# Second half's front in four slots a step of one tile each, with numbered beats and a third weight buffer

## The chip, the cores and the metric

The kernel runs on one core of a Trainium2 chip. Its time is that of one launch, in microseconds of the device. The core has TensorE (PE, matrix products into PSUM), VectorE (DVE), ScalarE (ACT), GpSimd (POOL) and SyncE (SP, here only a queue that issues DMAs), which run on their own and wait for each other by semaphores. All DMAs share 16 DMA engines.

## What is computed

One layer of a hybrid model over a prompt of 512 tokens and 8 single-token samples, D = 1024, float32.

```
h = modulate(rmsnorm(x), sh1, sc1);  proj = h @ w_in        -> u, z, xbc, dt, gates
ya = s5_branch(u);  ya = ya * sigmoid(ya @ w_glu + b_glu)   # "glu"
xs, B, C = silu(causal_conv(xbc))                           # "x": 2048 columns, 4 taps
yb = ssd(xs, dt, B, C, state)                               # chunks of 128 tokens; samples: one step each
yb = group_rmsnorm(yb * silu(z))
x  = x + gt1 * ((sigmoid(gA) * (ya @ w_branch_a) + sigmoid(gB) * (yb @ w_branch_b)) @ w_out)
h2 = modulate(rmsnorm(x), sh2, sc2)
# peer: 8 heads; q = h2 @ w_query; top 16 of 128 keys twice, top 16 of their 256 sums: 16 experts a head
y[t] = sum over 8 heads, 16 experts of  gelu(expert_down[e] . h2[t]) * g * expert_up[e]
x  = x + gt2 * y;  y_out = modulate(rmsnorm(x), shf, scf)
```

Each of 520 tokens thus reads 128 rows of 4 KB from `expert_down` and as many from `expert_up`.

## The kernel before

The program is a sequence of stages. The first ones (to about 630 us) make everything for the first 256 tokens (the "first half"), as far as the scores of head 0. The last one, `stage_peer`, is where the change lies; it starts near 630 us and lasts to the end.

**Gathers.** `stage_peer` has 32 units, one for each block of 128 tokens and head, plus one for the samples. A unit has two steps of eight experts. For each step GpSimd issues eight indirect DMAs that fetch 128 rows of `expert_down` (`gather_down`, L1706, 0.524 MB each) and eight of `expert_up` (`gather_up`, L1726); the up rows of step n - 4 (LAG) follow the down rows of step n. Down rows go to a ring of 10 buffers (12 after step 32, WIDE), up rows to eight buffers in one set, V. VectorE multiplies each down row by h2 and sums (`products`, L2366); ScalarE makes the gelu; VectorE makes the weights and finds the next unit's experts (`topk`); TensorE adds the up rows, four in each of two halves (`add`, L2035). GpSimd waits for an add's half before it fetches into those four V buffers. GpSimd's issues are strictly in order.

**The front.** The second half's (tokens 256 to 511, and the samples) whole way from `proj` to the scores has to be done before unit 16. It is written as four Python generators named `front`, one for each of TensorE, ScalarE and VectorE, and a straight list of loads on SyncE. Each `yield` ends a slot, and the loops over the units call `next(late)` at fixed places: TensorE three times a step (two, then the first half of `add(n - 4)`, then one, then the second half), ScalarE and VectorE six times a unit. So a slot is a third of a step. The order of the code is the order on the engine. In TensorE's front a slot is mostly `both`, which is two tiles (`product`, L2068): a tile is 8 matmuls of 128x128 weights with 264 columns. The pieces of weights, 1 MB each (8 x 256 columns, or 4 x 512), are in `order`: q (query projections of the first half), x, glu, gA, bra (branch a), z, gB, brb (branch b), wo, Q (query projections of the second half). TensorE's front has 75 slots: x and q 16, glu to z 14, tails 2, empty 2, the scan (`halves`, four times three slots) 12, then the norm, gB and brb 11, wo 4, empty 2, transposes 2, Q 9, and the samples' scores.

**Weights.** SyncE's `load(p)` (L1582) waits until the last tile of piece p - 2 is made, and loads into one of two buffers. `sample(b)` on SyncE (L1585 to L1595) stores a state when VectorE has updated it, loads B and C of sample b + 2, waits for the store, and loads state b + 2. On VectorE `sample(b)` is L2426 and L2431, on ScalarE `decay(b)` is L1772.

**The scan.** For each of four (chunk, half of the heads) TensorE makes the cumulative decays (L2169), B C products (L2174, L2177) and transposes of x (L2182) in two slots and the state product (L2188) and outputs (L2194, L2195) in the third. L2169 waits for VectorE's new state (L2521) of the last one, L2188 for VectorE's L2500 and L2506. L2200 transposes the final state, L2215 makes the group norms' sums, L2240 is the product with `w_out`, L2250 transposes h2 (which waits for L2583), L1229 are the scores, L1237 the samples' scores.

Of the kernel before, what the change touches and what calls it, by code (L numbers as in the profile page):

```python
# [93 lines left out]
class Map:  # L94
# [19 lines left out]
    S5_RING = KEEP + 2576  # L114
    SCR = KEEP + 2576
# [18 lines left out]
class Kept:  # L134


    def __init__(self, mem):
# [16 lines left out]
        self.carry = take(NCV, 3)  # L154
        assert M <= Map.SCR

# [213 lines left out]
def stage_mix(nc, mem, sem, ps, A, O, s_first):  # L370
# [5 lines left out]
    csv, tm, ex, vT, mask, hist, carry = kept.cs, kept.tm, kept.ex, kept.vT, kept.mask, kept.hist, kept.carry  # L376
# [18 lines left out]
    vT5 = mem(take(8), 8)  # L395
# [987 lines left out]
def pause(n):  # L1383
    for _ in range(n):
        yield


def stage_peer(nc, mem, sem, ps, A, O, mod_d, bc_d, keep_d, scale_d, integers):
# [36 lines left out]
    bglu = take(4)  # L1425
    bgn = take(P, rows=4)
# [11 lines left out]
    hist, carry = kept.hist, kept.carry  # L1438
    gt = [mem(Map.H2T + i * HW, HW) for i in range(4)]
# [3 lines left out]
    ring4 = [mem(Map.RING + i * KD * 256, 4, 512) for i in range(2)]  # L1443
# [3 lines left out]
    ecs, lm, cs_c = (mem(Map.SCR + i * D, 8, P) for i in range(3))  # L1447
    xdt, xdd = mem(Map.SCR + 3 * D, 8, HD), mem(Map.SCR + 3 * D + 512, 8, HD)
# [30 lines left out]
    WIDE = 2 * PH * 2  # L1479
# [3 lines left out]
    last = GATE * WIDE % NU1  # L1483
# [3 lines left out]
    for i in range(GATE * NSTEP):  # L1487
        s = i % NU1 if i < WIDE * GATE else ring2[(i - WIDE * GATE) % len(ring2)]
# [19 lines left out]
    order = ([("q", 1), ("x", 0), ("x", 1), ("x", 2), ("q", 2), ("x", 3), ("x", 4), ("x", 5), ("q", 3), ("x", 6), ("x", 7)]  # L1508
             + [("q", h) for h in range(4, PH)] + [("glu", 0), ("gA", 0), ("gA", 1), ("bra", 0), ("gA", 2), ("gA", 3), ("bra", 1)]
             + [("z", i) for i in range(4)] + [("gB", 0), ("gB", 1), ("brb", 0), ("gB", 2), ("brb", 1), ("gB", 3), ("brb", 2),  # L1510
                                               ("brb", 3)] + [("wo", i) for i in range(4)] + [("Q", h) for h in range(PH)])
    of_vector = ("bra", "brb", "wo")
    tiles_of = {"glu": 4, "bra": 4, "wo": 3}
    at_piece = {p: i for i, p in enumerate(order)}
    bank, made, free_at, gone, held = {}, {}, {}, {}, {}
    for name, i in order:
        for j in range(tiles_of.get(name, 2)):
            tile = (name, i, j)
            bank[tile] = 2 + (j if name == "wo" else j % 2)
            free_at[tile] = held.get(bank[tile])  # L1520
            made[tile] = len(made) + 1
            by = name in of_vector
            gone[tile] = 1 + sum((o[0] in of_vector) == by for o in gone)
            held[bank[tile]] = tile
# [1176 lines left out]
```

## Times and profile before

| | us |
|---|---|
| median of 3 runs | 2308.74 |
| lowest and highest | 2303.72, 2321.86 |
| the profiled execution's own time | 2309.2 |
| its span | 2307.4 |
| busy: TensorE, VectorE, GpSimd, ScalarE | 1310.1, 1433.8, 1008.2, 389.9 |

What a page calls the DMA share is the mean busy share of 16 DMA engines, which goes slightly over 1 when they are full. "a <- b" in the waits means that a stood idle until b. One `product` tile leaves 16 matmul records, half an `add` as many. PEclk and the granted clock are the mean of a stretch, 1 being 2.4 GHz.

### The profile page before, as it was taken

How to read it: one execution, taken by the hardware profiler on the slowest of the kernel's cores; microseconds unless marked ns; L12 is line 12 of the kernel's file. 1: busy time of each engine (PE TensorE's matmuls, PEld its weight loads, DVE VectorE, ACT ScalarE, POOL GpSimd, SP SyncE). 2: the span in 40 equal slices, each digit the busy share in tenths (PEclk: the TensorE clock that was granted, in tenths of full speed). 3: DMA queues.
4: the chain of work that ended last, by engine and by line, in shares of the span. 5: the costliest groups of instructions: out<-in, count | busy, mean ns of one | idle time of the engine just before them, and what ended most of it. 6: DMA issues, size and time to landing. Idle time of an engine off the chain costs nothing.

```text
span 2307.4 us, 20247 instructions
## 1 busy us (share of the span) xinstructions
PE 1310.1 (57%) x6421; PEld 762.5 (33%) x6421; DVE 1433.8 (62%) x3400; ACT 389.9 (17%) x859; POOL 1008.2 (44%) x1063
## 2 busy tenths in 40 slices
PE   3599994758768576545588685233322533323334
PEld 0178761545557454423365463000000100000000
DVE  0338999651368365587754744767866776776740
ACT  1011110430234122223210211100101111110100
POOL 0000000000034345365643646767776677777754
PEclk8799997779889788756799797655566655566557
DMA  9834320014287989997988998999998999999997
GB/s 366 329 97 146 109 73 18 16 60 167 96 310 282 341 317 390 327 380 292 363 323 318 382 346 333 414 413 413 413 413 336 397 400 413 413 413 413 413 360 290
DMA packets 249180, 697.75 MB, mean 302 GB/s; under 512 B 26751, under 2 KB 89891, under 8 KB 244935
## 3 DMA queue, kind: packets, MB, share of 16 engines
q0 software_dynamic: 149760, 545.33, 59.9%
q1 hardware_dynamic: 98490, 149.43, 18.2%
q10 hardware_dynamic: 824, 1.70, 0.2%
q8 instruction: 52, 0.85, 0.1%
q14 instruction: 54, 0.44, 0.1%
HBM read 687.36 MB, written 9.15 MB: 302 GB/s over the span
## 4 chain that ended last, share of the span: by engine, by line
DMA 19%; POOL 17%; PE 14%; issue 11%; DVE 9%; DVEq 1%; ACT 1%; SPq 0%; POOLq 0%; ACTq 0%
POOL arena L1706 9%; POOL arena L1726 8%; PE ps L2068 8%; DMA arena<-in_expert_up_dram,rows 5%; DMA arena<-in_expert_down_dram,expert 4%; DMA out_dram<-arena 3%; DVE arena L2366 3%; PE ps L2035 3%; DMA arena<-in_w_query_dram 2%; DMA arena<-in_w_in_dram 1%; DMA arena<-in_w_branch_b_dram 1%; DMA arena<-in_s_w_glu_dram 1%; PE ps L2240 1%; PE ps L2043 1%; DMA arena<-in_w_out_dram 1%
## 5 line engine op out<-in xcount | busy, mean ns | idle before, releaser
L2366 DVE CUSTOM_DVE_ANT_0 arena<-arena,ps 128x1024 f32<-128x1024 f32 x512 | 611.6, 1219 | 266.1 <-DMA arena<-in_expert_down_dram,expert 258.5
L2035 PE MATMUL ps<-arena 128*32 128x512 f32 x2048 | 378.5, 874 | 579.0 <-DMA arena<-in_expert_up_dram,rows 579.0
L1726 POOL DMA_INDIRECT arena<-in_expert_up_dram,rows x512 | 489.2, 955 | 424.2 <-PE ps L2035 259.8
L1706 POOL DMA_INDIRECT arena<-in_expert_down_dram,expert x512 | 490.1, 957 | 243.9 <-issue 149.5
L2068 PE MATMUL ps<-arena 128*128 128x264 f32 (+1 forms) x1344 | 343.3, 420 | 134.5 <-DMA arena<-in_w_in_dram 39.4
L2035 PEld LDWEIGHTS ps<-arena 128*32 128x32 f32 x2048 | 76.5, 140 | 824.1 <-issue 823.5
L2068 PEld LDWEIGHTS ps<-arena 128*128 128x128 f32 x1344 | 278.1, 210 | 201.8 <-issue 46.9
L650 PE MATMUL ps<-arena 128*128 128x256 f32 x640 | 141.8, 382 | 0.0
L650 PEld LDWEIGHTS ps<-arena 128*128 128x128 f32 x640 | 121.1, 191 | 23.3 <-issue 7.5
L1746 ACT ACTIVATE arena<-arena 128x8 f32<-128x8 f32 x65 | 13.5, 208 | 592.1 <-DVE arena L2366 592.0
L523 POOL MEMSET arena<- 16x1024 f32 x1 | 0.9, 941 | 239.4 <-DVE arena L936 239.4
L297 PE MATMUL ps<-arena 128*32 128x512 f32 x256 | 47.1, 873 | 45.6 <-DMA arena<-in_w_ada_dram 38.2
L722 PE MATMUL ps<-arena 128*32 128x512 f32 x64 | 39.8, 756 | 41.3 <-DVE arena L894 22.5
L1683 POOL MEMSET arena<- 128x1024 f32 x1 | 1.0, 956 | 125.9 <-POOLq L2670 125.9
L1746 ACT ACT_TABLE_LOAD x42 | 53.9, 1283 | 0.7
L1756 ACT ACTIVATE arena<-ps 32x32 f32<-32x32 f32 x64 | 13.8, 216 | 221.0 <-PE ps L2016 219.8
L510 POOL MEMSET arena<- 128x1024 f32 x1 | 1.0, 951 | 112.0 <-POOLq L2670 112.0
L2240 PE MATMUL ps<-arena 128*128 128x256 f32 (+1 forms) x192 | 42.8, 382 | 1.9 <-DMA arena<-in_w_out_dram 1.9
L2366 DVE DVE_READ_ACCUMULATOR2_ANT arena<- 128x1 f32 x520 | 42.9, 83 | 0.0
L1741 ACT ACT_TABLE_LOAD x33 | 42.3, 1283 | 1.8 <-PEq L2670 1.2
L2386 DVE TENSOR_TENSOR arena<-ps,arena 128x1024 f32<-128x1024 f32 (+1 forms) x4 | 4.9, 1219 | 57.2 <-PE ps L2035 56.6
L2314 DVE MAX8 arena<-arena 128x8 f32<-128x128 f32 (+1 forms) x99 | 33.6, 339 | 7.6 <-issue 0.4
(441 smaller groups left out, 1814.6 us busy)
## 6 DMA issues: line engine op xcount, KB each, us to landing
arena<-in_w_ada_dram SPq DMA_DIRECT2D x12, 2048.0 KB, 20.2
arena<-in_w_in_dram SPq DMA_DIRECT2D x11, 2048.0 KB, 7.6
arena<-in_w_in_dram SPq DMA_DIRECT2D x20, 1024.0 KB, 9.7
arena<-in_w_query_dram SPq DMA_DIRECT2D x16, 1024.0 KB, 15.6
arena<-in_w_ada_final_dram SPq DMA_DIRECT2D x4, 2048.0 KB, 16.2
arena<-in_w_out_dram SPq DMA_DIRECT2D x8, 1024.0 KB, 10.3
arena<-in_expert_down_dram,expert POOLq DMA_INDIRECT x512, 10.5
arena<-in_expert_up_dram,rows POOLq DMA_INDIRECT x512, 9.8
```

The source lines that it names most:

```text
L297: last = nc.tensor.matmul(ps[strip(j, 32), i, :], cT[:, k, :], ring[q][:, k % 2, 512 * j:512 * j + 512], start=(k == 0), stop=(k == KD - 1))
L650: last = mm(ps[:, 5 + n % 2, 0:HA], w, hA[:, k, 0:HA], start=(k == 0), stop=(k == KD - 1))
L722: last = mm(ps[32 * q:32 * q + 32, 7, :], CT[:, j, i, :], S_of(i)[j].rearrange("p a b -> p (a b)"), start=(j == 0), stop=(j == 1))
L1706: G.indirect_dma_start(U[i], None, down, bass.IndirectOffsetOnAxis(ap=at, axis=0))\
L1726: G.indirect_dma_start(Vr[r][j], None, up, bass.IndirectOffsetOnAxis(ap=at, axis=0))\
L1741: SE.activation(w[par], fv, ACT.Exp, bias=ssum[:, 1:2], accum_out=ssum[:, 0:1]).then_inc(s_exp, 1)
L1746: SE.activation(gel[n % 2], dots[n % 2], ACT.Gelu).then_inc(s_gelu, 1)
L2035: last = mm(ps[32 * j:32 * j + 32, c, :], Z[:, j, m, :], Vr[r][4 * half + j][:, c * 512:(c + 1) * 512], start=(p % 4 == 0 and m == 0), sto ...
L2068: last = mm(ps[:, bank[name, i, j], 0:n], w[:, k, j * P:(j + 1) * P], moving[:, k, 0:n], start=(k == 0), stop=(k == (3 if few else KD - 1)))
L2240: last = mm(ps[0:n, 2 + i, 0:256], mg[:, k, part], Q.ring[slot("wo", j)][:, k, :], start=(k == 0), stop=(k == KD - 1))
L2314: done(V.max(vals[:, 8:16], rep))
L2366: V.tensor_tensor_reduce(U[i], U[i], row, 1.0, 0.0, ALU.mult, ALU.add, dots[n % 2][:, j:j + 1]).then_inc(s_uused, 1)
```

## The change

The front is cut finer. Each generator counts its slots, now called beats, and `yield from until(beat)` leaves empty ones until the beat with that number; the units' loops call `next` four times a step on TensorE (two, half an add, two, half an add) and eight times a unit on ScalarE and VectorE. A `pair` puts one tile in each of two beats. TensorE's beats run from 0 to 134. VectorE's result of one beat is read by TensorE two or three beats later. Four weight slots take the place of two buffers: RA and RB as before, RM (a region free up to beat 29 and from h2 on) and RH (free until gB's sigmoids). RM is the third buffer in the x and q stretch and among the Q's, RH in the branch a and z stretch; from gB to brb there are two. `order` is changed in places: q2 comes after x1, q3 after x4, the tails come ahead of glu, and the gB pieces are made inside the scan, a tile at beats 57 + 5n and 59 + 5n, instead of between the brb's. The sigmoids of gB keep a buffer of their own (8 tiles), those of gA are written into `mg` and glu's into `yaB`. SyncE loads glu's weights before the B and C rows and puts the wait for a stored state (`again`) behind the next weight load. glu's bias comes from the stage before instead of a transposed load. The scan has five beats for each of its four turns, brb one beat a tile, wo three beats a piece. Products of the samples and their scales move a step or half a unit later, the ring of down rows grows at step 36 (MORE) instead of 32.

```diff
-    order = ([("q", 1), ("x", 0), ("x", 1), ("x", 2), ("q", 2), ("x", 3), ("x", 4), ("x", 5), ("q", 3), ("x", 6), ("x", 7)]
...
-             + [("z", i) for i in range(4)] + [("gB", 0), ("gB", 1), ("brb", 0), ("gB", 2), ("brb", 1), ("gB", 3), ("brb", 2),
-                                               ("brb", 3)] + [("wo", i) for i in range(4)] + [("Q", h) for h in range(PH)])
+    order = ([("q", 1), ("x", 0), ("x", 1), ("q", 2), ("x", 2), ("x", 3), ("x", 4), ("q", 3), ("x", 5), ("x", 6), ("x", 7)]
...
+             + [(name, i) for name in ("z", "gB", "brb", "wo") for i in range(4)] + [("Q", h) for h in range(PH)])
+    RA, RB, RM, RH = range(4)
+    slot_of = ([RB, RA, RM] * 5 + [RB, RA, RB, RA, RH, RB, RA, RH, RB, RA, RH] + [RB, RA] * 4
+               + [RB, RA, RH, RB] + [RA, RM, RB] * 2 + [RA, RM])
...
-                if p >= 2:
-                    sp.wait_ge(t_mm, last_of(*order[p - 2]))
...
+                if last_in[p] is not None:
+                    sp.wait_ge(t_mm, last_of(*order[last_in[p]]))
...
+            def again(b):
+
+                sp.wait_ge(t_h0w[b % 2], 16 * (b // 2))
+                load_state(b)
...
+                def until(beat):
+                    nonlocal now
+                    assert beat >= now, (beat, now)
+                    while now < beat:
+                        now += 1
+                        yield
...
-                both("x", 0, hB)
-                yield
-                both("x", 1, hB)
-                yield
...
+                yield from pair("x", 0, 1, hB)
+                yield from pair("x", 1, 3, hB)
...
-                    yield
+                    yield from until(57 + 5 * n)
+                    product("gB", n, 0, hB)
+                    yield from until(58 + 5 * n)
                     pe.wait_ge(t_cbm, n + 1)
                     pe.wait_ge(t_xdd, n + 1)
+                    pe.wait_ge(t_gone, gone["gB", n, 0])
...
+                for i in range(4):
+                    yield from pair("brb", i, 86 + 2 * i, cv)
+                yield from until(97)
...
                 if g != S:
                     next(late, None)
+                    next(late, None)
                 if n >= LAG:
                     add(n - LAG, 1)
...
-                    yield
+                    yield from until(58 + 5 * n)
                     dve.wait_ge(t_yps, n + 1)
...
+                yield from until(36)
+                sample(2)
...
+                yield from until(39)
+                sample(3)
```

Three places on the engines. First TensorE between two turns of the scan, before (L2169 starts a turn, L2188 is its state product, L2035 are the halves of adds):

```order
L2169 MATMUL ps<-arena 128x128 x8
L2174 MATMUL ps<-arena 128x128 x2
L2177 MATMUL ps<-arena 128x128 x2
L2035 MATMUL ps<-arena 32x512 x8
L2182 MATMUL ps<-arena 128x128 x4
L2035 MATMUL ps<-arena 32x512 x8
L2188 MATMUL ps<-arena 128x256 x2
```

and after (L2243 and L2265 stand for L2169 and L2188, L2094 for L2035, L2126 for L2068):

```order
L2243 MATMUL ps<-arena 128x128 x8
L2248 MATMUL ps<-arena 128x128 x2
L2251 MATMUL ps<-arena 128x128 x2
L2094 MATMUL ps<-arena 32x512 x8
L2256 MATMUL ps<-arena 128x128 x4
L2126 MATMUL ps<-arena 128x264 x8
L2094 MATMUL ps<-arena 32x512 x8
L2265 MATMUL ps<-arena 128x256 x2
```

The same two halves of adds lie between the start of a turn and its state product, and now also a tile of gB.

Second, TensorE where branch b is multiplied, before (L2068 are tiles of brb and gB, 16 matmuls being two tiles; L2240 is `w_out`):

```order
L2068 MATMUL ps<-arena 128x264 x32
L2035 MATMUL ps<-arena 32x512 x8
L2068 MATMUL ps<-arena 128x264 x16
L2035 MATMUL ps<-arena 32x512 x8
L2016 MATMUL ps<-arena 32x32 x4
L2068 MATMUL ps<-arena 128x264 x32
L2035 MATMUL ps<-arena 32x512 x8
L2068 MATMUL ps<-arena 128x264 x16
L2035 MATMUL ps<-arena 32x512 x8
L2240 MATMUL ps<-arena 128x256 x16
```

and after (L2126 are tiles of brb alone, L2312 is `w_out`):

```order
L2126 MATMUL ps<-arena 128x264 x16
L2094 MATMUL ps<-arena 32x512 x8
L2075 MATMUL ps<-arena 32x32 x4
L2126 MATMUL ps<-arena 128x264 x16
L2094 MATMUL ps<-arena 32x512 x8
L2126 MATMUL ps<-arena 128x264 x16
L2094 MATMUL ps<-arena 32x512 x8
L2126 MATMUL ps<-arena 128x264 x16
L2094 MATMUL ps<-arena 32x512 x16
L2075 MATMUL ps<-arena 32x32 x4
L2312 MATMUL ps<-arena 128x256 x8
```

Runs of four tiles and two between halves of adds have become runs of two, and two halves follow each other before `w_out`.

Third, SyncE's queue around the first samples, before (L1606 and L1589 write and read the B and C rows, L1585 loads a state, L1595 stores one, L1582 loads weights):

```order
L1606 DMA bc_scratch<-arena 8x1024
L1585 DMA arena<-in_state_ssm_dram 128x8x128
L1589 DMA arena<-bc_scratch 128x1024
L1585 DMA arena<-in_state_ssm_dram 128x8x128
L1589 DMA arena<-bc_scratch 128x1024
L1582 DMA arena<-in_s_w_glu_dram 128x4x512
L1582 DMA arena<-in_w_in_dram 128x8x256 x2
L1595 DMA out_dram<-arena 128x8x128
L1589 DMA arena<-bc_scratch 128x1024
L1585 DMA arena<-in_state_ssm_dram 128x8x128
```

and after (L1614, L1595, L1591, L1601 and L1588 in the same order):

```order
L1588 DMA arena<-in_s_w_glu_dram 128x4x512
L1614 DMA bc_scratch<-arena 8x1024
L1591 DMA arena<-in_state_ssm_dram 128x8x128
L1595 DMA arena<-bc_scratch 128x1024
L1591 DMA arena<-in_state_ssm_dram 128x8x128
L1595 DMA arena<-bc_scratch 128x1024
L1588 DMA arena<-in_w_in_dram 128x8x256
L1621 DMA out_dram<-arena 3x2048
L1622 DMA out_dram<-arena 8x2048
L1601 DMA out_dram<-arena 128x8x128
L1595 DMA arena<-bc_scratch 128x1024
L1588 DMA arena<-in_w_in_dram 128x8x256
```

The load of glu's weights has moved ahead of the B and C rows, and behind a state's store no load of a state follows directly.

## Rows read from the trace of the kernel before

**Rows 1.** Windows, core 0: busy us (x records) of five engines, granted clock, DMA share, GB/s.

```profile
640.00:740.00 100.00, 72.11 (x310) 59.54 (x309) 73.73 (x189) 36.18 (x83) 32.71 (x35) 0.86 0.80 284
740.00:960.00 220.00, 142.69 (x670) 103.02 (x672) 112.11 (x375) 51.20 (x124) 89.53 (x94) 0.81 0.93 347
960.00:1160.00 200.00, 110.60 (x647) 68.00 (x640) 161.30 (x402) 53.67 (x104) 114.06 (x116) 0.71 0.89 340
1160.00:1420.00 260.00, 204.71 (x1098) 144.51 (x1097) 137.64 (x336) 43.80 (x105) 128.33 (x135) 0.89 0.92 338
1420.00:1700.00 280.00, 95.12 (x501) 21.86 (x505) 198.49 (x492) 28.71 (x57) 203.98 (x215) 0.60 1.03 413
1700.00:2200.00 500.00, 166.80 (x836) 36.64 (x828) 359.59 (x882) 55.33 (x116) 362.50 (x380) 0.61 1.00 401
1320.00:1340.00 20.00, 17.32 (x92) 13.18 (x90) 13.48 (x40) 5.38 (x16) 12.04 (x13) 1.00 1.03 388
```

**Rows 2.** Waits, GpSimd, 640 to 1420 us: us in total, times, longest.

```profile
POOL arena L1726 <- PE ps L2035: 235.1, 29, 25.5
...
POOL arena L1706 <- DVE arena L2366: 39.4, 9, 12.5
```

**Rows 3.** Waits, TensorE, the same stretch.

```profile
PE ps L2068 <- DMA arena<-in_w_in_dram: 39.4, 7, 18.7
PE ps L2169 <- DVE arena L2521: 22.9, 3, 10.2
PE ps L2188 <- DVE arena L2506: 21.8, 4, 11.2
PE ps L2250 <- DVE arena L2583: 18.8, 1, 18.8
PE ps L2068 <- DMA arena<-in_s_w_glu_dram: 18.4, 1, 18.4
...
PE ps L2068 <- DMA arena<-in_w_query_dram: 15.0, 4, 5.3
...
PE ps L2068 <- DMA arena<-in_w_branch_b_dram: 12.8, 2, 6.8
```

**Rows 4.** Timeline, TensorE: start us, us, what, idle before and its releaser.

```profile
719.89 14.41 PE L2068 MATMUL ps<-arena 128*128 128x264 f32 x64
...
935.08 9.59 PE L2068 MATMUL ps<-arena 128*128 128x264 f32 x32 [18.74 <-DMA arena<-in_w_in_dram]
...
967.89 1.92 PE L2035 MATMUL ps<-arena 128*32 128x512 f32 x16
...
981.95 3.64 PE L2035 MATMUL ps<-arena 128*32 128x512 f32 x16 [7.06 <-DMA arena<-in_expert_up_dram,rows]
```

**Rows 5.** Timeline, GpSimd, issues of gathers.

```profile
961.48 0.94 POOL L1726 DMA_INDIRECT arena<-in_expert_up_dram,rows  x1 [25.48 <-PE ps L2035]
962.72 0.94 POOL L1726 DMA_INDIRECT arena<-in_expert_up_dram,rows  x1 [0.30 <-issue]
```

**Rows 6.** Page, DMA queues: packets, MB, share of 16 engines' span.

```profile
q1 hardware_dynamic: 98490, 149.43, 18.2%
```

**Rows 7.** DMA issues: count, KB each, median us to landing.

```profile
arena<-in_w_query_dram SPq DMA_DIRECT2D x16, 1024.0 KB, 15.6
...
out_dram<-arena SPq DMA_DIRECT2D x13, 512.0 KB, 19.6
...
arena<-in_state_ssm_dram SPq DMA_DIRECT2D x8, 512.0 KB, 5.3
...
arena<-in_w_branch_b_dram SPq DMA_DIRECT2D x4, 1024.0 KB, 15.3
```

**Rows 8.** Waits, SyncE's queue, 640 to 1420 us.

```profile
SPq L1585 <- DMA out_dram<-arena: 66.9, 6, 15.0
```

**Rows 9.** Lines, ScalarE, 640 to 1420 us: count, busy us, mean ns, idle before.

```profile
L1746 ACT ACT_TABLE_LOAD x22 | 28.2, 1283 | 0.4
L1772 ACT ACTIVATE arena<-arena 128x128 f32<-128x128 f32 x64 | 19.5, 388 | 9.0 <-DMA arena<-in_state_ssm_dram 9.0
```

More of the change, by code:

```diff
@@ L1515, in stage_peer @@
[L1515 to L1524, printed above, removed]
+    in_turn = ([(name, i, j) for name, i in order[:at_piece["gA", 0]] for j in range(tiles_of.get(name, 2))]
+               + [("gA", 0, 0), ("gA", 0, 1), ("gA", 1, 0), ("gA", 1, 1), ("bra", 0, 0), ("bra", 0, 1), ("gA", 2, 0),
+                  ("bra", 0, 2), ("bra", 0, 3), ("gA", 2, 1), ("gA", 3, 0), ("bra", 1, 0), ("bra", 1, 1), ("gA", 3, 1),
+                  ("bra", 1, 2), ("bra", 1, 3)]
+               + [(name, i, j) for name, i in order[at_piece["z", 0]:] for j in range(tiles_of.get(name, 2))])
@@ new lines, in stage_peer @@
+    bank, made, free_at, gone, held, turn = {}, {}, {}, {}, {}, {}
+    for tile in in_turn:
+        name, i, j = tile
+        if name in ("gA", "bra", "z", "brb"):
+            round_of = turn.setdefault(name == "brb", [])
+            bank[tile] = 2 + len(round_of) % 3
+            round_of.append(tile)
+        else:
+            bank[tile] = 3 - j if name == "gB" else 2 + j % 3 if name == "wo" else 2 + j % 2
+        free_at[tile] = held.get(bank[tile])
+        made[tile] = len(made) + 1
+        gone[tile] = 1 + sum((o[0] in of_vector) == (name in of_vector) for o in gone)
+        held[bank[tile]] = tile
@@ L1653, in _ @@
             sp.dma_start(shift2[2], mod_d[0:NS, 3 * D:4 * D]).then_inc(t_shift, 16)
-            for p in range(39, len(order)):
+            sp.wait_ge(t_h2, 3)
+            load(39)
+            for p in range(41, len(order)):
                 load(p)
@@ L1902, in front @@
-                yield from pause(2)
+                yield from until(26)
+                store(5)
+                keep(6, 0)
+                yield from until(27)
+                keep(6, 1)
+                yield from until(28)
+                store(6)
+                keep(7, 0)
+                yield from until(29)
+                keep(7, 1)
+                decay(0)
+                yield from until(30)
+                store(7)
+                tails(0)
+                yield from until(31)
@@ L2281, in _ @@
                     next(late, None)
+                    next(late, None)
                 if n >= LAG:
@@ L2634, in _ @@
                     topk(i + 1)
+                next(late, None)
                 weight(n)
```

689 lines of the change are left out of this document (360 added, 329 removed).

## Prediction

> **What bounds the kernel now.** I read the windows first, because the change touches one stage only. In [rows 1] the last two columns are what the DMA engines do. From 1420 us on they are full: share 1.03, 413 GB/s, and still 1.00 over the 500 us that hold the closings of blocks. That is the ceiling, and nothing in the change touches it. From 640 to 1420 us, while the second half's front runs between the gathers, the share is 0.80, 0.93, 0.89 and 0.92. Share times length is the DMA work of each stretch: 80.0, 204.6, 178.0 and 239.2 us, together 701.8. At 1.03 it would fit in 681.4 us of the 780. So 98.6 us is all that a perfect front could give; the rest of the program is worth nothing to this change.
>
> Next, who lets the queue run dry. GpSimd issues the gathers in order, and [rows 2] shows it waiting 235.1 us for TensorE's adds (L2035), against 39.4 us for VectorE's products. The eight V rows come free only when an add has run, and an add stands behind front work on TensorE. [rows 3] says what TensorE itself waits for there: weights (39.4 + 18.4 + 15.0 + 12.8 = 85.6 us), and VectorE's results (22.9 + 21.8 + 18.8 = 63.5 us). [rows 4] shows one such chain: 18.74 us for a weight tile at 935 us, and the gather that it holds up 25.48 us late in [rows 5].
>
> **Pace, counted in steps.** A step is eight gathers down and eight up. Before, TensorE has 75 front slots, three a step, so the front spans 25 steps; 780 / 25 = 31.2 us a step. After, it has 135 slots of at most one full tile (some smaller ones share a slot), four a step: 33.75 steps. So 8.75 steps of plain gathers, which now run after 1420 us, come to lie in the front. They cost no time of their own: 16 gathers of 0.524 MB are 8.39 MB, at 413 GB/s 20.3 us a step, 177.7 us in all, in either place.
>
> **The change part by part.**
>
> *Density on TensorE.* A tile takes 14.41 / 4 = 3.60 us in a run (16 records a tile), and 9.59 / 2 = 4.8 us behind a wait; half an add takes 1.92 us, and 3.64 us at the low clock [rows 4]. A dense step before is 6 x 3.60 + 2 x 1.92 = 25.4 us at best and 6 x 4.8 + 3.8 = 32.6 us behind waits. The DMA engines need 20.3 us for its gathers and, at 18.2% of 2307.4 us for 149.43 MB = 2.81 us a MB [rows 6], 8.8 us for three weight pieces of 1.05 MB: 29.1 us. So TensorE is beside or above the DMA. After, it has 4 x 3.60 + 3.8 = 18.2 to 4 x 4.8 + 3.8 = 23.0 us, and the DMA 20.3 + 5.9 = 26.2 us. The bound moves to the DMA in every dense step. GpSimd needs 16 x 1.24 = 19.8 us to issue a step [rows 5]: below both.
>
> *Weight buffers.* With two buffers a load has one piece of lead: two tiles and one or two adds, 9 to 14 us. The loads land in 15.6 (w_query) and 15.3 us (w_branch_b) in the median [rows 7]; the difference is the waits of [rows 3]. With three, up to beat 31, the lead is four tiles and two to three adds, above 18 us, so I take these waits as gone. In the branch b stretch the lead stays one piece (beat 87 frees what beat 90 reads), two tiles and two adds, 11 us against 15.3: up to 4 us twice, beside 12.8 us now.
>
> *SyncE's order.* The glu weights (18.4 us of waiting) are now loaded ahead of the B and C rows. Each wait for a stored state stands behind the next weight load instead of ahead of it; SyncE loses 66.9 us in six such waits [rows 8].
>
> *Two or three slots of distance.* In the scan stretch TensorE waits up to 11.2 us for L2506 (xdd, cbm) and up to 10.2 us for L2521 (the state). Two of a step's four slots are about 13 us at 26.9 us a step, so both should fall to a few us. The cost of it is length, counted above. The wait for h2 (18.8 us) gets two slots too.
>
> *What I cost at nothing.* ScalarE gets nine more table loads in program order (122 for 113), 1.283 us each [rows 9]; it is busy 36.2 + 51.2 + 53.7 + 43.8 = 184.9 of 780 us [rows 1]. Uncovered, 11.5 us. VectorE's extra drains, the transposed bias that goes away and the Q scores that become ready later (head 0 at slot 119, step 29.75; VectorE reads it in step 31) are hidden by the gathers. If the scores came late, VectorE would wait for two tiles, 7.2 us, once.
>
> **The sum.** First stretch: no add holds GpSimd back there, but VectorE's results do, and four tiles a step shorten that a little; I take share 0.85 (between 0.80 as now and 0.93 as in the next stretch): 80.0 / 0.85 = 94.1 us. The rest has 621.8 us of work, and 8.75 steps bring 177.7 x 1.03 = 183.0. For its share the bounds are 0.92 (as now in the densest stretch) and 1.03 (as after 1420 us). I take 0.99: just under the 1.00 of 1700 to 2200 us, where closings and the samples' step break in, and under the 1.03 of 1320 to 1340 us [rows 1], where weights and gathers run together and TensorE isn't behind. 804.8 / 0.99 = 812.9 us. Together 907.0 us, 26.9 us a step. Before, the same work took 780 + 177.7 = 957.7 us. The gain is 50.7 us, and 2309.2 - 50.7 = **2258.5 us**. The median shown is 2308.74, 0.5 us under the profiled execution's 2309.2; no correction.
>
> **A rule that speaks against it.** The clock first, by rows: over the front it is granted at 0.71 to 0.89, mostly the 2.4 GHz level, but at 0.60, mostly the 1.2 GHz level, once only adds run [rows 1], and a run of two tiles behind a wait takes 9.59 us where a run of four takes 7.2 us for two [rows 4]. The change cuts TensorE's runs from four and two tiles to two and two. The Trainium skill, "TensorE: Matmul & The Clock Gate", section "HAM oscillation — how this bites in real kernels", advises to bring dense work together, so that TensorE doesn't fall back to its half rate at each wait; by it thinner runs lose. That is the rival "clock" below.
>
> **The rivals.**
>
> *Fuller (0.09).* The rest reaches 1.03: 94.1 + 804.8 / 1.03 = 875.5 us, time 2227. For it: over the four stretches VectorE is busy 484.8, TensorE 530.1 and ScalarE 184.9 us of 780 [rows 1], so nobody else is near. Against: 0.524 MB transfers of states and rows arrive in bunches.
>
> *The samples' loop sets the pace (0.13).* State b+2 can't be loaded before state b is stored. One turn is the store, 19.6 us in the median, the load, 5.3 us [rows 7], eight passes of ScalarE, 8 x 0.388 = 3.1 us [rows 9], and eight of VectorE over tiles of the same size, as much: 31.1 us, with SyncE behind a weight load on top. It gets six slots, 40 us; before, it had two steps, 62 us. If each of the three turns on both buffers runs 8 us over, and half of that is covered, 3 x 8 = 24 us are lost: 2282. It decides from turns of 40 us on.
>
> *Nothing changes (0.09).* The eight V rows are what starves the queue, and waits for weights only turn into waits for V rows: 2309, or 2297 with a quarter of the gain. Against it: after 1420 us the same eight rows keep the share at 1.03.
>
> *Clock, the other side (0.06).* If TensorE's runs become slower in step with their thinness, it bounds the dense steps (slots 0 to 53, 86 to 108, 117 to 132: about 23 steps). A step is two runs and two adds at 3.64 us, 7.3 us. It decides from (26.9 - 7.3) / 2 = 9.8 us a run on; slower than now by over 1% from 11.4 us on. At 12 us a run a step is 31.3 us: 23 x 4.4 = 101 us, time 2360. The run behind the long wait here took 9.59 us, and the adds at 1.92 us stand right behind it, so it stays short of the edge.
>
> **How the numbers follow.** My forecast has 0.63. Its own range is 2242 to 2280 (share 1.01 to 0.965 in the second term). The range that should hold 8 in 10 goes from 2228, which leaves out about half of "fuller", to 2294, which leaves out most of "nothing changes" and all of "clock": 0.05 + 0.07 + 0.06, with the tails 0.2. This kernel's measurement tells about 1% (23 us) from no change. Faster by over 1% means under 2285.6: the forecast (0.62), fuller (0.09), half of the loop's (0.07): 0.78. Within 1%: 0.16. Slower by over 1%: 0.06.
>
> **What would show it.** TensorE's waits for weights in the front fall from 85.6 to under 15 us, those for L2506 and L2521 (under new line numbers) from 44.7 to under 15 us, and GpSimd's for adds from 235.1 to under 120 us over a front that is longer by about 130 us. The share between 740 us and the front's end is 0.97 to 1.01. The front's last scores on TensorE end near 640 + 907 = 1545 us. After them all stays at 413 GB/s. Wrong would be: a share that stays near 0.92 with GpSimd still waiting for adds (V rows), VectorE or ScalarE waiting for states or SyncE for stores longer than 66.9 us (the loop), or runs of two tiles over 9.8 us with a lower granted clock (clock).

## The result, and the profile after

The changed kernel takes 2261.18 us (median of four runs, 2254.31 to 2261.66) against 2309.94 us beside it: ratio 0.9766, 95% interval 0.9739 to 0.9793. A second set on one chip gave 2257.43 against 2310.57 us, 0.9761 (0.9738 to 0.9784). The forecast was 2258.5. The profiled execution took 2254.31 us, with this span and these busy times on its page:

```profile
span 2252.4 us, 20283 instructions
...
PE 1290.9 (57%) x6420; PEld 747.5 (33%) x6420; DVE 1431.3 (64%) x3400; ACT 401.8 (18%) x867; POOL 1010.9 (45%) x1063
```

Windows of the changed kernel, columns as in [rows 1]. The last row is everything from 740 us to the front's last scores on TensorE (L1238, which start at 1520.90 us); before, the scores (L1237) started at 1405.83 us.

```profile
640.00:740.00 100.00, 64.21 (x275) 51.70 (x276) 73.40 (x184) 33.67 (x76) 43.90 (x46) 0.80 0.84 310
740.00:840.00 100.00, 71.58 (x391) 49.02 (x389) 73.28 (x203) 36.34 (x80) 61.87 (x65) 0.91 1.04 395
840.00:940.00 100.00, 58.87 (x264) 38.86 (x264) 48.33 (x178) 11.45 (x28) 39.17 (x42) 0.79 0.98 365
940.00:1040.00 100.00, 54.11 (x265) 37.01 (x266) 47.55 (x180) 26.85 (x62) 32.13 (x34) 0.76 0.81 286
1040.00:1140.00 100.00, 67.98 (x432) 44.16 (x431) 83.90 (x194) 38.09 (x71) 71.50 (x73) 0.82 1.03 404
1140.00:1240.00 100.00, 54.17 (x314) 29.53 (x315) 84.71 (x189) 20.20 (x30) 67.00 (x69) 0.72 1.03 405
1240.00:1340.00 100.00, 70.75 (x336) 40.62 (x335) 60.44 (x159) 7.63 (x16) 57.68 (x62) 0.80 1.04 397
1340.00:1440.00 100.00, 60.91 (x323) 34.09 (x324) 77.39 (x186) 19.18 (x40) 64.70 (x68) 0.83 1.02 397
...
740.00:1521.00 781.00, 506.67 (x2689) 318.93 (x2689) 523.44 (x1405) 178.93 (x380) 441.76 (x460) 0.82 0.99 378
```

The forecast's share for that stretch was 0.99, and the last row has it. But no stretch runs at 0.99: the four windows from 1040 to 1440 us stand at 1.02 to 1.04, as full as plain gathers, and between 840 and 1040 us lies a hole, 0.98 and 0.81. At 1.03 those 200 us of windows would have held their work in (98 + 81) / 1.03 = 174 us: the hole is 26 us deep.

Waits of the changed kernel, 640 to 1560 us, one fence each for TensorE, GpSimd, VectorE and ScalarE. L2126 is the tile (L2068 before), L2094 the add (L2035), L1733 and L1753 are the gathers down and up (L1706, L1726), L2440 the products (L2366), L1799 the decay of a state on ScalarE (L1772), L2500 its use on VectorE, L2265 and L2243 the scan's matmuls (L2188, L2169).

```profile
PE ps L2094 <- DMA arena<-in_expert_up_dram,rows: 160.3, 29, 22.2
PE ps L2126 <- ACT arena L1829: 36.3, 3, 24.9
...
PE ps L2126 <- DMA arena<-in_w_in_dram: 10.8, 1, 10.8
...
PE ps L2265 <- DVE arena L2602: 6.7, 1, 6.7
```

```profile
POOL arena L1733 <- DVE arena L2440: 114.7, 33, 28.6
POOL arena L1753 <- PE ps L2094: 100.0, 29, 7.6
```

```profile
DVE arena L2500 <- ACT arena L1799: 80.1, 5, 31.9
```

```profile
ACT arena L1799 <- DMA arena<-in_state_ssm_dram: 114.4, 6, 33.2
```

GpSimd's 235.1 us for adds [rows 2] have become 100.0, and its 39.4 us for products 114.7. TensorE waits above all for the rows that its adds take (160.3 us): it is now ahead of the gathers, and DMA sets the pace outside the hole. What makes the hole is in the last two fences. One turn of it in four timelines, of SyncE's queue, ScalarE, VectorE and GpSimd (start us, us, what, idle before and its releaser):

```profile
913.68 0.38 SPq L1601 DMA_DIRECT2D out_dram<-arena  x1
...
964.12 0.62 SPq L1591 DMA_DIRECT2D arena<-in_state_ssm_dram  x1
```

```profile
990.59 2.44 ACT L1799 ACTIVATE arena<-arena 128x128 f32<-128x128 f32 x8 [28.54 <-DMA arena<-in_state_ssm_dram]
```

```profile
993.13 2.19 DVE L2500 SCALAR_TENSOR_TENSOR arena<-arena 128x128 f32<-128x128 f32 x8 [23.97 <-ACT arena L1799]
```

```profile
1000.41 0.94 POOL L1733 DMA_INDIRECT arena<-in_expert_down_dram,expert  x1 [16.21 <-DVE arena L2440]
```

State 3 is stored at 913.68 us. State 5, which goes into the same buffer, is asked for 50.4 us later and lands 26.5 us after that. Meanwhile ScalarE stands, VectorE stands behind it with the products of the next rows queued after the scan, and GpSimd has no free row to gather into. An engine that is busy 18% of the span stops the gathers.

Most of the 50.4 us is no work of the queue. SyncE's program has the next weight load ahead of the next sample and its reload, and that load waits for a tile of TensorE. First SyncE's waits for it between 840 and 1060 us, the longest of them ending at 961.65 us, then the run of tiles on TensorE that it waited for:

```profile
SPq L1588 <- PE ps L2126: 63.1, 5, 34.8
```

```profile
955.75 9.43 PE L2126 MATMUL ps<-arena 128*128 128x264 f32 x32 [24.91 <-ACT arena L1829]
```

L1829 is a sigmoid of gA on ScalarE, which itself stood 28.08 us for state 4 until 948.32 us. So a late state makes a tile late, the tile a weight load, and the weight load the next state.

### The profile page after: what moved, and what is told of

It reads as the page before. It is cut to its first block, busy times and chain, and to the rows that moved or that the text cites. A ratio compares the mean times of both kernels' runs of the same rounds, so it can differ in the third digit from the quotient of the medians.

```text
span 2252.4 us, 20283 instructions
## 1 busy us (share of the span) xinstructions
PE 1290.9 (57%) x6420; PEld 747.5 (33%) x6420; DVE 1431.3 (64%) x3400; ACT 401.8 (18%) x867; POOL 1010.9 (45%) x1063
## 4 chain that ended last, share of the span: by engine, by line
DMA 26%; POOL 14%; DVE 11%; issue 9%; PE 8%; ACT 2%; SPq 1%; DVEq 1%; POOLq 0%; ACTq 0%
DMA arena<-in_expert_up_dram,rows 14%; POOL arena L1753 7%; POOL arena L1733 7%; DMA arena<-in_expert_down_dram,expert 6%; DMA arena<-in_state_ssm_dram 5%; DVE arena L2440 5%; PE ps L2094 4%; PE ps L2126 3%; DMA arena<-in_w_branch_b_dram 1%; SPq L1595 1%; ACT arena L1799 1%; DVE arena L2487 1%; DVEq L2381 1%; DMA arena<-in_expert_down_dram,sample 1%; PE ps L2312 1%
## 5 line engine op out<-in xcount | busy, mean ns | idle before, releaser
L2440 DVE CUSTOM_DVE_ANT_0 arena<-arena,ps 128x1024 f32<-128x1024 f32 x512 | 609.4, 1217 | 248.7 <-DMA arena<-in_expert_down_dram,expert 239.7
L2094 PE MATMUL ps<-arena 128*32 128x512 f32 x2048 | 367.6, 852 | 605.6 <-DMA arena<-in_expert_up_dram,rows 597.7
L1733 POOL DMA_INDIRECT arena<-in_expert_down_dram,expert x512 | 491.8, 961 | 325.1 <-issue 139.9
L1753 POOL DMA_INDIRECT arena<-in_expert_up_dram,rows x512 | 490.1, 957 | 283.5 <-issue 147.9
L2126 PE MATMUL ps<-arena 128*128 128x264 f32 (+1 forms) x1344 | 340.9, 414 | 91.2 <-ACT arena L1829 36.3
L2094 PEld LDWEIGHTS ps<-arena 128*32 128x32 f32 x2048 | 75.0, 136 | 832.0 <-issue 823.5
L2126 PEld LDWEIGHTS ps<-arena 128*128 128x128 f32 x1344 | 271.4, 206 | 167.8 <-ACT arena L1829 38.0
L651 PEld LDWEIGHTS ps<-arena 128*128 128x128 f32 x640 | 120.5, 190 | 23.5 <-issue 7.5
L298 PE MATMUL ps<-arena 128*32 128x512 f32 x256 | 45.9, 854 | 46.5 <-DMA arena<-in_w_ada_dram 37.6
L2500 DVE SCALAR_TENSOR_TENSOR arena<-arena 128x128 f32<-128x128 f32 x64 | 17.5, 345 | 80.1 <-ACT arena L1799 80.1
L723 PE MATMUL ps<-arena 128*32 128x512 f32 x64 | 41.3, 782 | 36.0 <-DVE arena L895 20.0
L2312 PE MATMUL ps<-arena 128*128 128x256 f32 (+1 forms) x192 | 45.9, 397 | 0.0
L2440 DVE DVE_READ_ACCUMULATOR2_ANT arena<- 128x1 f32 x520 | 42.5, 82 | 0.0
L1799 ACT ACTIVATE arena<-arena 128x128 f32<-128x128 f32 x64 | 19.5, 388 | 114.4 <-DMA arena<-in_state_ssm_dram 114.4
## 6 DMA issues: line engine op xcount, KB each, us to landing
arena<-in_w_ada_dram SPq DMA_DIRECT2D x12, 2048.0 KB, 19.4
```

Of the source, the lines that this page charges most:

```text
L298: last = nc.tensor.matmul(ps[strip(j, 32), i, :], cT[:, k, :], ring[q][:, k % 2, 512 * j:512 * j + 512], start=(k == 0), stop=(k == KD - 1))
L651: last = mm(ps[:, 5 + n % 2, 0:HA], w, hA[:, k, 0:HA], start=(k == 0), stop=(k == KD - 1))
L723: last = mm(ps[32 * q:32 * q + 32, 7, :], CT[:, j, i, :], S_of(i)[j].rearrange("p a b -> p (a b)"), start=(j == 0), stop=(j == 1))
L1733: G.indirect_dma_start(U[i], None, down, bass.IndirectOffsetOnAxis(ap=at, axis=0))\
L1753: G.indirect_dma_start(Vr[r][j], None, up, bass.IndirectOffsetOnAxis(ap=at, axis=0))\
L1799: last = SE.activation(h0[b % 2][:, k, :], h0[b % 2][:, k, :], ACT.Copy, scale=ex[:, k, 8 + b:9 + b])
```

## The experiments

Ratios are to the kernel before, on the same chip. The first four runs and the last four stood beside a kernel before of 2313.53 and 2310.57 us; the middle four ran on a slower chip, where it took 2439.69 us.

**States ahead of weights.** Each reload of a state goes ahead of the next sample's store and of the weight load behind that. One weight load still stands between a state's store and its reload:

```
             load(17)
+            again(2)
             sample(1)
             load(18)
-            again(2)
             sp.wait_ge(t_tlw, 32)
             load(19)
+            again(3)
             sample(2)
```

> The changed kernel with SyncE's list around the samples in another order: the load of state b is issued ahead of the store of state b - 1 and of the B and C rows and weights that follow, instead of behind them. Theory A (the samples' loop holds the front back because a state's load stands behind about 1.5 to 2 MB in SyncE's own queue): ScalarE's waits for states fall from 114.4 us to under 50 us, the DMA share between 840 and 1040 us rises from 0.90 to at least 0.98, and the time falls by 15 to 25 us, to 2236 to 2246 (ratio to before about 0.970). Rival B (the states land late because the 16 engines are full of gathers, wherever they stand in the queue): landing times stay at 13 to 28 us, and the time stays within 5 us of 2261 (ratio 0.975 to 0.979).

Measured: 2236.55 us, ratio 0.9666 (0.965 to 0.9682), 24.6 us under the changed kernel. The share between 840 and 1040 us is 1.05 and 0.98, as expected. ScalarE's waits for states fall from 114.4 to 73.2 us only, not to under 50. The landing median of a state hardly changes (20.3 us for 19.4), so it is the loads' place in SyncE's program that counted, not their speed. From the issue of a state's store to that of the reload of its buffer, six times in each timeline of SyncE's queue, the mean is 20.5 us in the kernel before, 38.4 us in the changed kernel and 26.3 us here (in the second run of this version, below). The order has a price too: TensorE now waits 20.2 us, once, for weights of branch a.

**Two buffers in x and q again.** Only the x and q pieces alternate between two again:

```
-    slot_of = ([RB, RA, RM] * 5 + [RB, RA, ...
+    slot_of = ([RB, RA] * 7 + [RB] + [RB, RA, ...
```

> The changed kernel with the third weight buffer taken out of the x and q stretch (slots 0 to 31), everything else as it is. Theory A (the third buffer is what ended TensorE's waits for weights, and they cost time): those waits rise from 10.8 us by 20 to 40 us, and the time by 10 to 20 us, to 2271 to 2281 (ratio 0.981 to 0.985). Rival B (one tile a slot already gives the loads time; the buffer is idle help): waits rise by some us, the time by 0 to 4 us (ratio 0.976 to 0.979).

Measured: 2268.54 us, 0.982 (0.9794 to 0.9846): 7.4 us of the gain are gone by the medians, 12 by the ratios, less than Theory A's 10 to 20 by the one and inside it by the other. TensorE's waits for weights rise only from 14.2 to 22.5 us, where Theory A had 20 to 40 us more. In its timeline TensorE waits for weights three times between 740 and 810 us, 7.50, 2.00 and 1.27 us:

```profile
752.74 6.02 PE L2126 MATMUL ps<-arena 128*128 128x264 f32 x16 [7.50 <-DMA arena<-in_w_in_dram]
```

**Six slots a step.** The same slots, six in a step instead of four, so the front is as dense as before; one load of h2 moves with it:

```
-                for _ in range(4):
+                for _ in range(6):
                     next(late, None)
                 gelu(step_of[2 * u + 1])
-                for _ in range(2):
+                for _ in range(3):
                     next(late, None)
```

> The changed kernel with six one-tile slots a step instead of four on TensorE and twelve a unit instead of eight on ScalarE and VectorE, so the tiles are as dense as before; the buffers, the order of pieces and the distances in slots stay (a row's load on SyncE moves so that nothing blocks). The front is then 22.5 steps. Theory A (the lower density is what moved the bound from TensorE to the DMA): the share in the front falls back to 0.92 to 0.95, GpSimd waits again over 180 us for adds, and the time is 2285 to 2300 (ratio 0.989 to 0.996). Rival B (buffers, order and distances did it, the density is free): 2255 to 2265 (ratio 0.975 to 0.980).

Measured: 2277.13 us, 0.9835 (0.9815 to 0.9855), between both. GpSimd's waits for adds are 141.5 us over 640 to 1540 us:

```profile
POOL arena L1753 <- PE ps L2094: 141.5, 32, 17.6
```

So four slots a step instead of six are worth some 16 us of the 54 that a ratio of 0.9766 means here; the other 38 us come with the buffers, the order and the distances, also in a dense front. The 16 us are not density alone: six slots a step also shorten, in time, the lead of every weight buffer and the distance of two or three slots, and TensorE waits 14.1 us for h2 here. No run tells these apart. That the adds wait this much less than before in a front just as dense (235.1 in [rows 2]) says that TensorE's waits, not its work alone, held the adds up.

**Before, with the third buffer alone.** Nothing else of the change:

```
+    three = [1, 0, 2] * 5
+    slot_of = [three[p] if p < 15 else (p + 1) % 2 for p in range(len(order))]
```

> The kernel before with one part of the change alone: a third weight buffer for its first 15 pieces (x and q). Theory A (the parts work only together; in this stretch before, few of the waits are for these pieces, and the dense slots stay): the time falls by 0 to 8 us (ratio 0.9965 to 1.000). Rival B (the buffer is the part that pays): 15 to 30 us faster (ratio 0.987 to 0.9935).

Measured: 2304.3 us, 0.9962 (0.9947 to 0.9976), 9.2 us. That is just above Theory A's 0 to 8 us and agrees with the second run: the third buffer in x and q is worth some 7 to 12 us. GpSimd's 235.1 us for adds hardly move (219.3, over 640 to 1540 us):

```profile
POOL arena L1738 <- PE ps L2047: 219.3, 27, 26.3
```

**On the slower chip.** Glu weights behind the B and C rows again; the scan's results used in the next slot instead of two or three later; and two on the states, first with packets of 4 KB, then, on top of the first experiment, with seven of the eight stores issued by ScalarE:

```
-            for p in range(1, 16):
+            for p in range(1, 15):
                 load(p)
...
+            load(15)
             load(16)
```

> The changed kernel with one thing undone: the load of glu's weights stands on SyncE behind the B and C rows and the first two states again. Theory A (the early load is worth its wait): TensorE waits 10 to 20 us for glu's weights at slot 32, and the time rises by 8 to 15 us (ratio 0.980 to 0.983, against the changed kernel's 0.977). Rival B (with the engines full, slot 32 is late enough for either order, or the samples behind gain what glu loses): within 4 us (ratio 0.975 to 0.979).

```
-                    yield from until(56 + 5 * n)
+                    yield from until(56 + 3 * n)
                     pe.wait_ge(t_seg, n + 1)
```

> The changed kernel with the scan packed into three slots a turn, so that VectorE's result of one slot is read in the next, as before; gB's tiles stay in the scan, and the slots behind it are left empty, so that the front's length stays. Theory A (the distance of two slots removed the waits, and these held gathers back): TensorE's waits for VectorE in the scan (now 6.7 and 3.3 us) rise to 35 to 60 us, the DMA share there falls from 1.03 to about 0.93, and the time rises by 5 to 12 us (ratio 0.979 to 0.982). Rival B (the waits come back but the gathers' buffers cover them): the time stays within 3 us (ratio 0.975 to 0.9785).

```
-                sp.dma_start(h0[b % 2], A["state_ssm"][0, b].rearrange("(k q) p n -> (q p) k n", q=2))
+                sp.dma_start(mem(Map.SCR + (b % 2) * D, D), A["state_ssm"][0, b].rearrange("h (a c) n -> (h a) (c n)", a=8))
```

> The changed kernel with the samples' states loaded and stored in runs of 4 KB instead of 512 bytes for each partition, the same bytes; the states of the samples then lie in wrong places, so y_sample and the samples' states are not computed rightly. Theory A (the engines take packets of SyncE's queue and of the gathers in turn, so a transfer in 512-byte packets gets a ninth of the bytes beside 4 KB gathers): landing of a state falls from 19.4 us to under 10 us, ScalarE's waits for states from 114.4 us to under 50 us, and the time by 12 to 25 us, to 2236 to 2249. Rival B (what counts is bytes ahead in SyncE's queue, and not the packets' size): landing over 15 us, time within 6 us of 2261.

```
                 def decay(b):
+                    if b:
+                        act.wait_ge(t_hnew, b)
+                        act.dma_start(O[8][0, b - 1].rearrange(...), h0[(b - 1) % 2]).then_inc(t_h0w[(b - 1) % 2], 16)
                     act.wait_ge(t_h0[b % 2], 16 * (b // 2 + 1))
```

> The kernel of e1_states_first with the states' stores issued from ScalarE's queue instead of SyncE's. Theory A (each queue gets its turn of packets, so the stores go beside SyncE's loads and not in line with them): a state's load is no longer behind a store, ScalarE's waits for states fall from 73.2 to under 45 us, and the time by 4 to 12 us against e1 (ratio 0.961 to 0.965 to before). Rival B (all queues share the same full engines, and ScalarE loses as much by waiting for VectorE before it issues): within 3 us of e1, or slower (ratio 0.965 to 0.970).

Measured: 2375.1 us, 0.9725 (0.9678 to 0.9771), for the glu weights; 2397.7, 0.9824 (0.9778 to 0.987), for the next slot; 2349.48, 0.9623 (0.957 to 0.9676), with 4 KB packets; 2338.55, 0.9575 (0.9529 to 0.9621), with ScalarE's stores. The changed kernel did not run on this chip. The last two were run again on the faster one (below) and stood 0.004 and 0.005 higher there, so the changed kernel would be near 0.972 here. The glu load's place then moves nothing that can be seen (its own wait was 18.4 us in [rows 3]; in that run TensorE has no wait for glu's weights, where 10 to 20 us were expected). The next slot is 22.6 us slower than the kernel with the late glu load, on this same chip: that is what the distances are worth, if the glu load is worth nothing.

How they are worth it is not what was expected. TensorE's waits for VectorE in the scan were to rise to 35 to 60 us and are 0.4. The state product (L2264 in this run) waits for ScalarE's sigmoid of a gB tile (L1832), which is now made in the slot just before:

```profile
PE ps L2264 <- ACT arena L1832: 23.0, 3, 15.0
```

But the kernel with the late glu load, whose scan is that of the changed kernel, has 19.6 us of the same wait on this chip. What the 22.6 us consist of is open; the windows show where they lie, a share of 0.78 and 0.87 from 1040 to 1240 us against 0.91 and 0.97 with the late glu load.

With 4 KB packets and with ScalarE's stores the ratios come out even lower than Theory A had them, but ScalarE's waits for states do not: they are 78.5 and 78.0 us, where under 50 and under 45 were expected.

**The four that matter, on one chip.** The changed kernel, states first, ScalarE's stores, and 4 KB packets:

> The changed kernel itself once more, so that what stands beside it in this set is measured on the same chip. On the first chip its ratio to the kernel before was 0.977. If the second chip's slower gathers (361 to 373 GB/s in their plain stretch, where the first chip's ran at 409) change only the scale, the ratio here is 0.972 to 0.981; if that chip made every version gain more, as the ratios of the last set alone could be read, it is 0.965 to 0.971.

> The version with each state load ahead of the x/q and gate weights, on the same chip as the changed kernel. Theory A (the samples' loop costs the changed kernel about 25 us because its state loads are late): again 20 to 30 us under the changed kernel, ratio 0.964 to 0.969 to the kernel before. Theory B (that difference was one of chips or days): within 8 us of the changed kernel.

> The same with seven of the eight state stores issued by ScalarE on its own queue. Theory A (what a state load or store waits for is its place in SyncE's queue of small packets, which gets one packet for each large one of the gathers, so a second small queue doubles the share): 5 to 15 us under the version with states first, ratio 0.957 to 0.963. Theory B (the 16 engines are full, so another queue only divides them anew): within 4 us of the version with states first, and the low ratio of the last set was that chip's.

> The changed kernel with each state moved in packets of 4 KB instead of 512 B, in a flat layout, so that the states' values stand in the wrong places and outputs 1 and 8 are not the reference's. Theory A (packets of 512 B alternate one for one with the gathers' large ones, and 4,096 of them a sample take up the queue): 15 to 30 us under the changed kernel, ratio 0.962 to 0.970. Theory B (bytes alone count, and they are the same): within 6 us of the changed kernel.

| kernel | us | ratio, 95% interval |
|---|---|---|
| changed | 2257.43 | 0.9761, 0.9738 to 0.9784 |
| states first | 2233.10 | 0.9663, 0.9639 to 0.9687 |
| states first, stores from ScalarE | 2226.67 | 0.9628, 0.9611 to 0.9646 |
| changed, 4 KB packets (samples' states in wrong places) | 2232.44 | 0.9662, 0.9642 to 0.9682 |

The changed kernel is where it was, and the last two ratios are 0.005 and 0.004 above those of the slower chip: the low ratios there were the chip's. States first is 24.3 us under the changed kernel, 24.6 the first time. Its windows, and those of ScalarE's stores, from 740 us to the start of the scores (1501 and 1497 us):

```profile
940.00:1040.00 100.00, 69.24 (x359) 45.05 (x358) 58.95 (x177) 28.13 (x62) 54.81 (x57) 0.84 0.98 366
...
740.00:1501.00 761.00, 502.89 (x2702) 318.60 (x2704) 526.38 (x1409) 181.33 (x383) 443.21 (x463) 0.83 1.02 390
```

```profile
740.00:1497.00 757.00, 511.31 (x2717) 321.33 (x2716) 527.55 (x1412) 181.46 (x383) 447.26 (x465) 0.83 1.03 393
```

The hole is all but gone (0.98 for 0.81), and the front reaches the ceiling, though ScalarE still waits 69.8 us for states: what is left of these waits is covered. Stores from ScalarE bring 6.4 us more; the four runs of either kernel don't overlap (2224.23 to 2227.41, 2230.03 to 2238.69). This version is the fastest of all, 3.7% under the kernel before. It does not get its states sooner, as was expected; its waits for them are longer than the 69.8 us:

```profile
ACT arena L1804 <- DMA arena<-in_state_ssm_dram: 82.2, 7, 28.7
```

Packets of 4 KB bring 25.0 us without any change of order, with the same bytes. Why, the next rows show. First the changed kernel, DMA queues between 845 and 862 us, while GpSimd gathers and SyncE moves states and B and C rows (packets, MB, share):

```profile
q0 software_dynamic: 1448, 5.27, 77.2%
q1 hardware_dynamic: 1451, 1.59, 26.2%
```

Both queues moved as good as the same number of packets, 1448 and 1451, and so they did in the same 17 us in the four kernels of this set (1475 and 1473, 1480 and 1484, 1407 and 1403, 1267 and 1269), whatever the size: they take turns. A gather's packet is 3.64 KB, one of SyncE's 1.10 KB, so SyncE gets 94 GB/s of 405. Over 640 to 1560 us the queue has 62,854 packets in the changed kernel and 48,518 with rows of 4 KB, 896 fewer for each of the 16 transfers of states: 1,024 packets a transfer against 128 (my expectation had 4,096 a sample; it is 2,048). At one turn each, a state in rows of 512 B passes while 1,024 x 3.64 KB = 3.7 MB are gathered.

That is not all of the 25.0 us. From 740 us to the scores (1526 and 1498 us) SyncE's queue moves 53.2 MB in 20.3% of 786 us in the changed kernel and 53.1 MB in 19.6% of 758 us with 4 KB packets, 160 against 149 us. So some 11 us are the small packets' own time on the engines, in a front where the engines are full. The rest is the hole, which is not closed here: shares of 1.01 and 0.93 between 840 and 1040 us make it 12 us deep, for 27 in the changed kernel of this set. ScalarE's waits for states fall from 120.1 to 91.6 us, not to under 50.

Now SyncE's own timeline, L1595 being the load of B and C rows, three of its eight; first the changed kernel (the trace of the first set), then 4 KB packets:

```profile
798.62 12.48 SPq L1595 DMA_DIRECT2D arena<-bc_scratch  x1
...
826.28 10.79 SPq L1595 DMA_DIRECT2D arena<-bc_scratch  x1
...
850.33 13.17 SPq L1595 DMA_DIRECT2D arena<-bc_scratch  x1
```

```profile
798.84 0.43 SPq L1595 DMA_DIRECT2D arena<-bc_scratch  x1
...
830.12 0.42 SPq L1595 DMA_DIRECT2D arena<-bc_scratch  x1
...
843.30 0.32 SPq L1595 DMA_DIRECT2D arena<-bc_scratch  x1
```

The same instruction holds SyncE 10.8 to 13.2 us in these places behind a state in small packets, and 0.3 to 0.4 us behind one in large ones. The other five of the changed kernel took 0.3 to 1.4 us, also behind states in small packets, so it is no fixed price. Where it is paid, whatever stands after it, a reload of the next state among it, goes out so much later. The landing medians of states (8 loads) say the rest, changed kernel in this set first, 4 KB packets second:

```profile
arena<-in_state_ssm_dram SPq DMA_DIRECT2D x8, 512.0 KB, 20.1
```

```profile
arena<-in_state_ssm_dram SPq DMA_DIRECT2D x8, 512.0 KB, 13.8
```

The Trainium skill, "DMA: Bandwidth & Descriptors", section "Queues, rings and completion order", says that a DMA engine goes round the queues that have work for it, a packet at a time, and means by a packet a group of descriptors, typically 9 to 17. The 1448 and 1451 packets agree with turns of equal length; a packet of the profile is one row here (1,024 for a state), and how many of them make a turn these counts can't say.

With ScalarE's stores there are three queues. Between 865 and 870 us, in the run on the faster chip, GpSimd's moved 431 packets (1.57 MB), SyncE's 430 (0.22 MB) and ScalarE's 429 (0.22 MB). Each has its own turn, so the stores do pass beside SyncE's loads. The Trainium skill's same page, section "Rules for kernel authors", calls it no help to spread DMAs over issuing engines, save for the time on the issuer. Here ScalarE's stores gave 6.4 us. Whether these come from the third turn or from SyncE's time at issue no run tells; that they come from earlier states, the 82.2 us of waits speak against.

## Why the prediction came out right, and where it did not hold

The time was right to 2.7 us, and that closely by luck, because two terms went the other way than forecast and cancelled: a front fuller than forecast, and a hole 26 us deep in it. By the steps:

- **The ceiling and the stretch before it.** Held: the first 100 us stand at 0.84 (taken: 0.85).
- **Density on TensorE.** Held in direction: most runs of two tiles take 7.4 us (next row), DMA sets the pace outside the hole. The forecast gave it no size of its own; six slots a step show that density, with the time that it gives to buffers and distances, is some 16 us.

```profile
1226.62 7.39 PE L2126 MATMUL ps<-arena 128*128 128x264 f32 x32
```

- **Weight buffers.** Waits for weights fell from 85.6 to 14.2 us (10.8 for w_in, and 3.4 for branch b in two waits, as feared; forecast under 15). The third buffer is worth 7 to 12 us in x and q by two runs.
- **Two or three slots of distance.** L2602 and L2617 cost 6.7 and 3.3 us (forecast under 15). Worth 22.6 us by two runs on the slower chip, but not through the waits that I named: without the distances the waits for VectorE stay at 0.4 us.
- **SyncE's order: the step that failed.** I wrote that each wait for a store now stands behind the next weight load, counted that as relief for SyncE (66.9 us of waits in [rows 8]), and gave it no price. Those waits stood directly ahead of the reload: from a state's store to the reload of its buffer took 20.5 us before and 38.4 after, where the reload stands behind weight loads that wait for TensorE (63.1 us, 34.8 at once). SyncE's waits for stores are indeed gone, but 68.4 us of waits for VectorE's updated state (13.3 before) stand in their place. Moving the reloads forward, ahead of one of these weight loads, gives 24.3 and 24.6 us. The order of the kernel before, the reload directly behind the wait, was not run in the changed kernel.
- **The share 0.99 for the rest: right as a mean, wrong as a reason.** I set it under 1.03 for closings and the samples' step after 1420 us. It is 1.02 to 1.04 over 400 us, 1.02 over the whole stretch with states first. The rival "fuller" described the front, less the hole.
- **The samples' loop, given 0.13.** It occurred beside the forecast: its sign, waits for states on ScalarE and VectorE, is there with 114.4 and 80.1 us. That its price was 24 us and the effect of the reloads' place 24.3 us is luck, since the price was of three turns that run 8 us over. I took a turn as 31.1 us, with the load at the 5.3 us of [rows 7]. That median is of moments in which hardly a gather ran: between 856.5 and 862 us, around such a load, SyncE's queue had 1050 packets and the gathers' 145. In the changed kernel the load lands in 19.4 us, behind a weight load of its own queue and beside gathers that take every other turn (1788 and 1785 packets between 970 and 990 us). And SyncE's program stands between store and reload, which I named and did not price: 38.4 us from store to reload instead of the 19.6 of the store alone. Decays on the same buffer start at 887.8 and 948.3, and at 908.9 and 990.6 us: turns of 60.5 and 81.7 us against 40 available. "SyncE behind a weight load on top" was the larger part of the turn.
- **GpSimd's waits for adds.** 100.0 us (forecast under 120). That the waits for products would grow from 39.4 to 114.7 us was not said.
- **End of the front.** I put the scores near 1545, at the end of a stretch that was cut at 1420 us, while before they stood at 1405.8. From there the forecast is 1533; measured 1520.9. The remainder after the scores then took 731.5 us, where the forecast leaves 2307.4 - 1405.8 - 177.7 = 723.9. So the front was 11.9 us shorter than forecast and the rest 7.6 us longer, which again cancels in part.
- **Clock.** The rival did not occur: the granted clock from 740 us to the scores is 0.82, mostly the 2.4 GHz level, as before (0.81), with runs half as long, and the time fell. Runs of two tiles took 7.1 to 10.0 us; one, behind a wait for branch b, passed the 9.8 us that I had named. The Trainium skill ("TensorE: Matmul & The Clock Gate", "HAM oscillation — how this bites in real kernels") advises against thin runs between waits; the trace does not show that cost here.

By the runs: 7 to 12 us for the third buffer, some 16 for the thinner front, 22.6 for the distances, of 54 us in all. The pieces overlap and each is known to some 5 to 10 us, so this is a scale and not a balance; what the order of the pieces and the third buffers outside x and q are worth no run isolates. And 24 us more were there to be had.

## What to carry to other kernels

A landing time read while the other queues are idle is no price for the same transfer once the change has filled them: take it from the fullest stretch, and count the instructions of its queue between the event that frees a buffer and the reload, with what each of them waits for. When a front is made to fill the queue, put the loads of a loop that carries its own dependence ahead of bulk loads that wait for a buffer, look at what the bulk loads then cost (20.2 us, once, here), and move small-row transfers in the largest packets that the layout allows. A total that comes out right needs the windows beside it: a mean of 0.99 was 1.03 and a hole.

## What was not expected of the hardware

- Beside gathers, SyncE's queue got one packet for one (1451 to 1448 in 17 us), 94 of 405 GB/s with packets of 1.1 KB against 3.64 KB; a third queue, ScalarE's, got as many again (431, 430, 429 in 5 us).
- Three of eight loads of B and C rows held SyncE for 10.8 to 13.2 us when states went in rows of 512 B; the same three took 0.3 to 0.4 us when the states went in rows of 4 KB.
- The same 53 MB of SyncE's queue took 160 us of the engines' time with states in rows of 512 B and 149 us with rows of 4 KB.
- One chip ran the kernel before in 2439.69 us and another in 2310.57, 5.6% apart, and changed versions gained 0.4 to 0.5 of a per cent more on the slower one. What makes the chip slower is open.
